# Two blocks of a transformer on one core: first conditioning pieces into the slab, ranks between the shared expert's halves, its down product in pair 14

## The chip, the core and the metric

The program runs on one core of a Trainium2 chip. The metric is the time of one execution on the device in microseconds. The kernel before took 2307.77 us in the median of three runs (2303.73 to 2310.81).

## The reference

256 tokens of width 1024, float32, pass through two blocks of two layers each. In the first block each layer is

```python
mod = silu(c) @ ada_w[layer] + ada_b[layer]
sh1, sc1, g1, sh2, sc2, g2 = split(mod, 6)
h = x * (1 + sc1) + sh1
y = mixer(h)                       # layer 0: block attention and gated linear attention; layer 1: gated delta rule
x = layer_norm(ALPHA * x + g1 * y)
h = x * (1 + sc2) + sh2
s = sigmoid(h @ router_w)          # 64 experts, top 6 of each token, limited to 4 of 8 groups
y = sum over a token's experts e of share_e * down_e(silu(gate_e h) * up_e h)
y = y + sh_down(silu(sh_gate h) * sh_up h)      # the shared expert, for all tokens
x = layer_norm(ALPHA * x + g2 * y)
```

The second block (attention with context and a pool mixer, then a Hyena and a Fourier mixer) follows on the same tokens. The change does not touch it.

## The kernel before

All weights come from HBM as pieces of 128 x 2048 float32, 1024 KB each. SP issues nearly all loads, in the order of the program and from one queue, into numbered buffers: four of `wbuf` (`NS = 4`) in the mixers, nine in the experts' stage (four of `wbuf`, two more of it, two of the slab, and `wP`). `load` takes the next buffer in turn and first waits until the work that held it is done; all later loads wait behind it. POOL issues the conditioning pieces of later sections on a queue of its own, into the two remaining pieces of `wbuf`.

**Conditioning.** `ada_w` is 12 sections for the first block, each of four pieces. VectorE multiplies a piece by its column of the activated condition and adds it up, two instructions a piece, eight a section (`ada_steps`). TensorE then sums over the partitions (`ada_pe`) and VectorE adds the bias (`ada_dve`). Sections 0 and 1 (shift and scale of the first layer) are summed at the start; SP loads their eight pieces with `load`, so the fifth waits for the first buffer. Sections 2 to 7 (`E_ADA`) are summed in the even mixer, a few steps at a time between the copies of the projections, with `some(steps, n)`. `ada_pool` issues each of their pieces when the one two before it has been summed.

**Start and even mixer.** VectorE makes h from x in eight pieces (`start_dve`), and one signal tells that all are made. `even_pe` first multiplies the table of relative position biases (33 x 4 by 512, `e_tab`), waits for that signal, then runs 13 projections of 256 columns (the last of 16), each 16 matrix products, and in the fourth, seventh, ninth and twelfth place after them an `ada_pe`. VectorE copies the bias table out first of all (L775), and POOL sends it through memory (`even_pool`) to lay it out as `hank`, which the scores need, and only then starts with section 2. After the projections come scores, softmax (with one conditioning step after each of its eight rounds), gated linear attention and the output product.

**Experts' stage** (`moe_sp`, `moe_pe`, `moe_act`, `moe_dve`), once a layer, at 264 to 830 us and 1242 to 1808 us. TensorE's order: router, transposes of h, gate and up products of the shared expert in two halves m (`m_sh`), the sums of the experts' places (`m_rank`), the shared down product into the accumulators `Y`, three gathers (`gather_pe`), then 32 pairs of experts. VectorE's order: the router's choice, the shared expert's two products silu(gate) times up (L1242), ranks (L974 on), two sets of places (`places_dve`, L311 and L1018), copies of the gathers. A gather needs its set of places. Pair q: gate and up of both experts, four pieces (L300), the scatter of pair q-1 into `Y`, transposes (L304), in the first nine pairs one more gather, and the down product from two pieces. ScalarE copies the rows of pair q+1 (`window_act`) while pair q runs.

In the trace one matrix product of `mm` is two records. L300 is the line of `mm`, L304 that of `tr`, L311 and L312 those of `ts`, L431 the conditioning sum.

## Time and profile before

| | |
|---|---|
| median of three runs | 2307.77 us |
| the profiled execution | 2311.57 us, its span 2309.7 us |
| TensorE products | 2039.2 us busy, 88% |
| VectorE | 814.7 us, 35% |
| ScalarE | 448.1 us, 19% |
| DMA | 577 MB, mean 250 GB/s |
| chain that ended last | PE 76%, DVE 10%, DMA 6%, issue 4% |

The page gives the whole; the change sits in three short stretches of it. So the views are read for those stretches: busy time of each engine by stage, the timeline around each edit, and for a transfer its issue, the time to its landing and the first instruction that reads it. A stage in which TensorE is busy without a gap can only lengthen if work is put into it; in one in which it waits, what it waits for decides.

### The profile page before, as it was taken

What the parts mean: (1) busy time and instruction counts of PE and PEld (TensorE: products, weight loads), DVE (VectorE), ACT (ScalarE), POOL (GpSimd) and SP (SyncE); (2) the same over time, 40 slices, a digit from 0 to 9 for tenths busy, and PEclk for the clock granted to TensorE, in tenths of its full rate; (3) what the DMA queues carried; (4) which work ended last, traced back from release to release, by engine and by line L of the source; (5) the groups of instructions that cost most, each with busy time, mean ns of one, the idle gap of its engine ahead of it and who ended that gap; (6) DMA issues with size and microseconds to landing.
All of it is one profiled execution on the core that took longest, in us unless ns stands there. A gap on an engine that the chain in (4) does not pass through costs nothing.

```text
span 2309.7 us, 24377 instructions
## 1 busy us (share of the span) xinstructions
PE 2039.2 (88%) x9590; PEld 1392.7 (60%) x9590; DVE 814.7 (35%) x1728; ACT 448.1 (19%) x982; POOL 84.8 (4%) x101
## 2 busy tenths in 40 slices
PE   5967899999999979958988999999999797779987
PEld 4856755554444458838977555444444585547856
DVE  4562353210111027668623622110111353551262
ACT  0013212112221221140022111212221403221021
POOL 0100000000000000010000000000000000020050
PEclk9976899999999989958988999999999898889999
DMA  9860278899999936863002788999999472112401
GB/s 368 327 252 7 90 309 332 355 386 405 407 411 410 407 144 252 302 250 110 1 23 86 302 355 356 383 409 407 406 413 407 190 291 73 32 55 74 146 21 37
DMA packets 80098, 576.99 MB, mean 250 GB/s; under 512 B 8925, under 2 KB 9181, under 8 KB 10529
## 3 DMA queue, kind: packets, MB, share of 16 engines
q1 hardware_dynamic: 68976, 494.84, 53.6%
q0 software_dynamic: 10992, 80.43, 9.5%
q8 instruction: 81, 1.33, 0.2%
q14 instruction: 49, 0.39, 0.0%
HBM read 574.17 MB, written 1.06 MB: 249 GB/s over the span
## 4 chain that ended last, share of the span: by engine, by line
PE 76%; DVE 10%; DMA 6%; issue 4%; ACT 2%; POOL 1%; POOLq 0%; SPq 0%; DVEq 0%; ACTq 0%
PE ps L300 75%; DMA wbuf<-in_ada 6%; DVE hma L431 4%; PE ps L304 2%; ACT slab L307 1%; DVE slab L311 1%; ACT L307 1%; POOL rs_t L2108 0%; POOL hma L2107 0%; DVE hma L312 0%; DVE slab L1018 0%; DVE slab L2263 0%; DVE slab L312 0%; POOL hma L2110 0%; DVE stat L1962 0%
## 5 line engine op out<-in xcount | busy, mean ns | idle before, releaser
L300 PE MATMUL ps<-slab 128*128 128x256 f32 (+5 forms) x2544 | 588.4, 405 | 29.0 <-issue 13.8
L300 PEld LDWEIGHTS ps<-slab 128*128 128x128 f32 (+2 forms) x2544 | 407.5, 186 | 186.7 <-issue 140.7
L307 ACT ACTIVATE slab<-ps 128x512 f32<-128x512 f32 (+3 forms) x282 | 148.2, 526 | 1290.5 <-PE ps L300 1278.5
L300 PE MATMUL ps<-wbuf,slab 128*64 128x512 f32 (+1 forms) x1392 | 349.9, 590 | 26.5 <-issue 26.5
L300 PE MATMUL ps<-hma,wbuf 128*128 128x256 f32 (+1 forms) x1648 | 368.0, 386 | 1.2 <-DVE hma L312 1.2
L300 PEld LDWEIGHTS ps<-hma,wbuf 128*128 128x128 f32 (+1 forms) x1648 | 317.2, 193 | 49.5 <-DVE hma L312 3.2
L300 PE MATMUL ps<-slab,cst 128*64 128x512 f32 (+3 forms) x554 | 187.0, 553 | 63.7 <-ACT slab L307 30.8
L300 PEld LDWEIGHTS ps<-wbuf,slab 128*64 128x64 f32 (+1 forms) x1392 | 122.5, 138 | 192.6 <-issue 191.8
L1264 DVE TENSOR_TENSOR slab<-ps,slab 128x256 f32<-128x256 f32 x64 | 27.2, 425 | 591.3 <-ACT slab L307 571.0
L431 DVE SCALAR_TENSOR_TENSOR hma<-wbuf,cs,hma 128x1024 f32<-128x1024 f32 x140 | 179.6, 1283 | 72.2 <-DMA wbuf<-in_ada 68.6
L300 PE MATMUL ps<-wbuf,cst 128*64 128x512 f32 x704 | 191.0, 592 | 0.0
L300 PEld LDWEIGHTS ps<-slab,cst 128*128 128x128 f32 (+1 forms) x554 | 93.2, 190 | 125.3 <-issue 79.2
L300 PE MATMUL ps<-wP,slab 128*64 128x512 f32 (+2 forms) x440 | 159.6, 484 | 8.9 <-DVE wP L1955 8.9
L300 PE MATMUL ps<-slab,wbuf 128*128 128x256 f32 x616 | 138.9, 388 | 11.9 <-DVE slab L879 8.8
L300 PEld LDWEIGHTS ps<-slab,wbuf 128*128 128x128 f32 x616 | 119.7, 195 | 32.3 <-issue 15.6
L300 PEld LDWEIGHTS ps<-wbuf,cst 128*64 128x64 f32 x704 | 65.9, 137 | 93.2 <-issue 92.9
L1269 DVE COPY slab<-ps 128x512 f32<-128x512 f32 x64 | 44.2, 691 | 202.5 <-PE ps L304 202.5
L304 PE MATMUL ps<-cst,slab 128*128 128x128 f32 x380 | 61.8, 297 | 36.0 <-DVE slab L311 12.4
L307 ACT ACTIVATE slab<-slab 128x512 f32<-128x512 f32 (+2 forms) x146 | 70.6, 509 | 104.5 <-DVE slab L580 85.3
L300 PEld LDWEIGHTS ps<-wP,slab 128*64 128x64 f32 (+1 forms) x440 | 62.9, 161 | 40.8 <-issue 30.5
L304 PEld LDWEIGHTS ps<-cst,slab 128*128 128x128 f32 x380 | 50.4, 154 | 48.4 <-issue 25.8
L300 PE MATMUL ps<-wbuf,hma 128*128 128x256 f32 (+2 forms) x256 | 56.5, 390 | 23.8 <-issue 15.9
(250 smaller groups left out, 1392.2 us busy)
## 6 DMA issues: line engine op xcount, KB each, us to landing
wbuf<-in_moe_gu SPq DMA_DIRECT2D x170, 1024.0 KB, 8.5
wbuf<-in_moe_d SPq DMA_DIRECT2D x88, 1024.0 KB, 10.3
wbuf<-in_ada POOLq DMA_DIRECT2D x72, 1024.0 KB, 5.7
slab<-in_moe_gu SPq DMA_DIRECT2D x64, 1024.0 KB, 8.6
wbuf<-in_od_in SPq DMA_DIRECT2D x30, 1024.0 KB, 4.9
wbuf<-in_ev_in SPq DMA_DIRECT2D x22, 1024.0 KB, 8.2
wP<-in_moe_gu SPq DMA_DIRECT2D x22, 1024.0 KB, 9.3
slab<-in_moe_d SPq DMA_DIRECT2D x20, 1024.0 KB, 10.3
```

The costliest lines, as they stand in the source:

```text
L300: return e.matmul(o, lhsT, rhs, start=start, stop=stop, skip_group_check=skip)
L304: return e.transpose(o, i, ident[0:n, 0:n])
L307: return e.activation(o, i, fn, bias=bias, scale=scale, accum_out=acc)
L311: return e.tensor_scalar(o, a, s1, None, op0)
L431: t = e.scalar_tensor_tensor(total, w, cs[:, c, k:k + 1], total, ALU.mult, ALU.add)
L1264: e.tensor_tensor(m_hh[:, q % 2, :], bank("m_gu", l, q)[:, 256:512], m_sg[:, q % 2, :], ALU.mult).then_inc(*V.up("m_hh", l, q))
L1269: e.tensor_copy(m_tp[:, q % 2, :], bank("m_tt", l, q)[:, :]).then_inc(*V.up("m_ttc", l, q))
```

## The change

The first eight conditioning pieces go to the slab, which is empty then, each with a semaphore of its own, without waiting for a buffer and ahead of x; the constants are loaded behind the second projection's weights. POOL issues the pieces of sections 2 and 3 as soon as the condition vector is made, ahead of the bias table's way through memory. Each of the eight pieces of h has a signal, and projection 0 waits for them one by one. The bias table's product and its copy move behind projection 3. In the experts' stage the sums of places stand between the two halves of the shared expert's gate and up; VectorE makes the second shared product between the first and the second set of places, and writes both to a free part of `hma`. The down product moves into pair 14, after the scatter, and its load to the place ahead of pair 14's loads. The first scatter opens the accumulators in its stead.

```diff
@@ -17,6 +17,7 @@
 ALPHA = float(4 ** 0.25)
 CAP = 64
 NC = 6
+SHARED_AT = 14

...
-        def proj_f(e, key, n, rhs, freed_by):
+        def proj_f(e, key, n, rhs, freed_by, ready=None):
             u = unit(key, 8, n)
             p = fill_bank(e, key, freed_by)
             e.wait_ge(*on("landed", key))
             for m in range((n + 127) // 128):
                 w = min(128, n - m * 128)
                 for k in range(8):
+                    if ready is not None and m == 0:
+                        e.wait_ge(*on(*ready(k)))
                     i = mm(e, p[0:w, m * 256:(m + 1) * 256], u[:, k, m * 128:m * 128 + w], rhs[:, k, :], k == 0, k == 7)
             i.then_inc(*P.up(*key))
             P.also("used", key)
...
         def ada_at(n, q):
-            return flat(unit(("ada", n, q), 1, 2048)) if n < 2 else wbuf[:, 4 + q % 2, :]
+            return S(4 * n + q, 2048) if n < 2 else wbuf[:, 4 + q % 2, :]

...
-                    V.also("used", ("ada", n, q))
+                    V.also("ada_used", n, q)
...
-        def ada_pool(e, tasks, *ready):
-            for x in ready:
-                e.wait_ge(*on(*x))
+        def ada_pool(e, tasks, first=True):
             for n in tasks:
                 for q in range(4):
-                    if n > tasks[0] or q > 1:
-                        e.wait_ge(*on("used", ("ada", n - (q < 2), (q + 2) % 4)))
+                    if n > tasks[0] or q > 1 or not first:
+                        e.wait_ge(*on("ada_used", n - (q < 2), (q + 2) % 4))
                     e.dma_start(wbuf[:, 4 + q % 2, :], A["ada"][TASKS[n][0], q]).then_inc(
                         *G.arrive(f"ada_w{q % 2}", ("ada", n, q)))
...
         def start_sp(e):
             e.dma_start(tab[:, :], A["table"]).then_inc(*Q.arrive("in_tab", "tab_in"))
-            e.dma_start(flat(xT[:, :, :]), A["xT"]).then_inc(*Q.arrive("in_x", "x"))
             for n in range(2):
                 for q in range(4):
-                    load(e, ("ada", n, q), A["ada"][n, q])
-            e.dma_start(cst[:, 0:lo], A["consts"][:, 0:lo]).then_inc(*Q.arrive("in", "in"))
+                    e.dma_start(ada_at(n, q), A["ada"][n, q]).then_inc(*Q.arrive(f"in_a{4 * n + q}", ("ada", n, q)))
+            e.dma_start(flat(xT[:, :, :]), A["xT"]).then_inc(*Q.arrive("in_x", "x"))
...
             for j in range(8):
-                i = ts(e, hT[:, j, :], xT[:, j, :], mc(0, 1, j), mc(0, 0, j), ALU.mult, ALU.add)
-            i.then_inc(*V.up("e_h"))
+                ts(e, hT[:, j, :], xT[:, j, :], mc(0, 1, j), mc(0, 0, j), ALU.mult, ALU.add).then_inc(*V.up("e_h", j))
             e.wait_ge(*V.now)
             ts(e, xT[:, :, :], xT[:, :, :], ALPHA, None, ALU.mult).then_inc(*V.up("x_scaled"))
...
         def even_sp(e):
             for i in range(12):
+                if i == 2:
+                    e.dma_start(cst[:, 0:lo], A["consts"][:, 0:lo]).then_inc(*Q.arrive("in", "in"))
                 load(e, ("e_proj", i), A["ev_in"][i])
             load(e, ("e_proj", 12), A["ev_glr"])
             load_out(e, "e_out", A["ev_out"])
...
         def even_pe(e):
-            p = fill_bank(e, ("e_tab",), ("e_tabc",))
-            e.wait_ge(*on("landed", "in"))
-            mm(e, p[0:4, :], rpe33, K("hot")[0:33, :], True, True).then_inc(*P.up("e_tab"))
-            e.wait_ge(*on("e_h"))
+            proj_f(e, ("e_proj", 0), 256, hT, ("e_ev", 0), lambda k: ("e_h", k))
             for i, (c0, n, f) in enumerate(E_UNITS):
-                (proj_f if f else proj_t)(e, ("e_proj", i), n, hT, ("e_ev", i))
+                if i:
+                    (proj_f if f else proj_t)(e, ("e_proj", i), n, hT, ("e_ev", i))
+                if i == 3:
+                    p = fill_bank(e, ("e_tab",), ("e_tabc",))
+                    e.wait_ge(*on("landed", "in"))
+                    mm(e, p[0:4, :], rpe33, K("hot")[0:33, :], True, True).then_inc(*P.up("e_tab"))
                 if i in (4, 7, 9, 12):
                     ada_pe(e, {4: 2, 7: 3, 9: 4, 12: 5}[i])
             for q in range(8):
...
         def even_dve(e):
-            e.wait_ge(*on("e_tab"))
-            e.tensor_copy(rs_t[0:4, 0, :], bank("e_tab")[0:4, :]).then_inc(*V.up("e_tabc"))
-
             def proj(i, dst, rows=128, cols=512, tokens=False):
                 e.wait_ge(*on("e_proj", i))
                 p = bank("e_proj", i)[0:rows, 0:cols]
@@ -786,6 +786,8 @@
                 *V.up("e_ev", 1))
             some(steps, 5)
             proj(3, flat(e_qk[:, 6:8, :]))
+            e.wait_ge(*on("e_tab"))
+            e.tensor_copy(rs_t[0:4, 0, :], bank("e_tab")[0:4, :]).then_inc(*V.up("e_tabc"))
             some(steps, 3)
             proj(4, e_v[:, :, 0:256], tokens=True)
             some(steps, 3)
...
-        m_sh = S(6, 2048)[:, 768:1792].rearrange("p (a n) -> p a n", a=4)
+        m_sh = S(6, 2048)[:, 768:1280].rearrange("p (a n) -> p a n", a=2)
+        m_shh = hma[:, 1:3, 1600:1856]
         m_htok = S(0, 2, 1024)
...
             if q == 1:
-                e.wait_ge(*on("m_shy", l))
+                e.wait_ge(*on("m_shv", l, 1))
...
             for j in range(8):
-                t = mm(e, Y(j), m_ys[:, q % 2, j * 128:j * 128 + 128], m_tp[:, q % 2, 256:512], False, q == NP - 1 and j % 2 == 1, True)
+                t = mm(e, Y(j), m_ys[:, q % 2, j * 128:j * 128 + 128], m_tp[:, q % 2, 256:512],
+                       q == 0 and j % 2 == 0, q == NP - 1 and j % 2 == 1, True)
             t.then_inc(*P.up("m_y", l, q))
...
         def moe_sp(e, l, before):
             load(e, ("m_rt", l), A["router"][l])
             load(e, ("m_shg", l), A["sh_gu"][l, 0])
             load(e, ("m_shu", l), A["sh_gu"][l, 1])
-            load(e, ("m_shd", l), A["sh_d"][l])
             slots.ids, slots.i = [slots.ids[(slots.i + i) % NS] for i in range(NS)] + list(range(NS, 9)), 0
             for s in range(NS, 9):
                 slots.held.pop(s, None)
             for q in range(NP):
+                if q == SHARED_AT:
+                    load(e, ("m_shd", l), A["sh_d"][l])
                 for part in (0, 4, "d"):
                     for x in (2 * q, 2 * q + 1):
                         key = ("m_w", l, x, part)
@@ -1106,6 +1111,26 @@
...
             slots.ids, slots.i = list(range(NS)), 0
             over(e, l, over_sp, Q)
 
+        def ranks_pe(e, l):
+
+            p = fill_bank(e, ("m_rank", l), ("m_rankr", l))
+            e.wait_ge(*on("m_msk", l))
+            mm(e, p[:, 0:64], K("before"), r_msk[:, 0, :], True, True)
+            mm(e, p[:, 64:128], ones, r_msk[:, 0, :], True, False)
+            mm(e, p[:, 64:128], K("before"), r_msk[:, 1, :], False, True)
+            mm(e, p[:, 128:192], ones, r_msk[:, 0, :], True, False)
+            mm(e, p[:, 128:192], ones, r_msk[:, 1, :], False, True).then_inc(*P.up("m_rank", l))
+
+        def shared_pe(e, l):
+            u = unit(("m_shd", l), 2, 1024)
+            e.wait_ge(*on("m_shv", l, 1))
+            e.wait_ge(*on("landed", ("m_shd", l)))
+            for kk in range(2):
+                for j in range(8):
+                    t = mm(e, Y(j), u[:, kk, j * 128:j * 128 + 128], m_shh[:, kk, :], False, False, True)
+            t.then_inc(*P.up("m_shy", l))
+            P.also("used", ("m_shd", l))
+
         def moe_pe(e, l, h):
 
             p = fill_bank(e, ("m_log", l), ("m_exp", l))
@@ -1125,6 +1150,8 @@
                         t = tr(e, p[:, k * 128:k * 128 + 128], hT[:, 4 * k2 + k, m * 128:m * 128 + 128])
                     t.then_inc(*P.up("m_ht", l, m, k2))
             for m in range(2):
+                if m:
+                    ranks_pe(e, l)
                 p = fill_bank(e, ("m_sh", l, m), ("m_shv", l, m))
                 for half, key in ((0, ("m_shg", l)), (1, ("m_shu", l))):
                     u = unit(key, 8, 256)
@@ -1135,23 +1162,7 @@
                     t.then_inc(*P.up("m_sh", l, m, half))
                     if m == 1:
                         P.also("used", key)
-
-            p = fill_bank(e, ("m_rank", l), ("m_rankr", l))
-            e.wait_ge(*on("m_msk", l))
-            mm(e, p[:, 0:64], K("before"), r_msk[:, 0, :], True, True)
-            mm(e, p[:, 64:128], ones, r_msk[:, 0, :], True, False)
-            mm(e, p[:, 64:128], K("before"), r_msk[:, 1, :], False, True)
-            mm(e, p[:, 128:192], ones, r_msk[:, 0, :], True, False)
-            mm(e, p[:, 128:192], ones, r_msk[:, 1, :], False, True).then_inc(*P.up("m_rank", l))
             take_y(e, ("y_res", f"m{l}"))
-            e.wait_ge(*on("m_shv", l, 1))
-            u = unit(("m_shd", l), 2, 1024)
-            e.wait_ge(*on("landed", ("m_shd", l)))
-            for kk in range(2):
-                for j in range(8):
-                    t = mm(e, Y(j), u[:, kk, j * 128:j * 128 + 128], m_sh[:, 2 + kk, :], kk == 0 and j % 2 == 0, False, True)
-            t.then_inc(*P.up("m_shy", l))
-            P.also("used", ("m_shd", l))
 
             e.wait_ge(*on("m_htc", l, 1, 1))
             for n in range(3):
@@ -1178,6 +1189,8 @@
                 P.also("m_gu", l, q, 1)
                 if q:
                     scatter_pe(e, l, q - 1)
+                if q == SHARED_AT:
+                    shared_pe(e, l)
                 p = fill_bank(e, ("m_tt", l, q), ("m_ttc", l, q))
                 e.wait_ge(*on("m_hh", l, q))
                 for i in range(2):
@@ -1237,12 +1250,15 @@
 
         def moe_dve(e, l):
             router_dve(e, l)
-            for m in range(2):
+            def shared(m):
                 e.wait_ge(*on("m_shs", l, m))
-                e.tensor_tensor(m_sh[:, 2 + m, :], bank("m_sh", l, m)[:, 256:512], m_sh[:, m, :], ALU.mult).then_inc(
+                e.tensor_tensor(m_shh[:, m, :], bank("m_sh", l, m)[:, 256:512], m_sh[:, m, :], ALU.mult).then_inc(
                     *V.up("m_shv", l, m))
+
+            shared(0)
             ranks_dve(e, l)
             places_dve(e, l, 0)
+            shared(1)
             places_dve(e, l, 1)
             for n in range(2):
                 gather_dve(e, l, n)
@@ -1790,7 +1806,8 @@
         def attn_pool(e):
             e.wait_ge(*on("m_gu", 1, NP - 1, 1))
             e.dma_start(cst[:, lo:], A["consts"][:, lo:]).then_inc(*G.arrive("c2", "late"))
-            ada_pool(e, A_ADA, ("n_c", "m1", 0))
+            e.wait_ge(*on("n_c", "m1", 0))
+            ada_pool(e, A_ADA)
 
         def attn_pe(e):
             rstd_pe(e, "ax", S(7, 8, 256))
@@ -2355,8 +2372,9 @@
         def pool_program(e):
             start_pool(e)
             e.wait_ge(*on("ca"))
+            ada_pool(e, E_ADA[0:2])
             even_pool(e)
-            ada_pool(e, E_ADA)
+            ada_pool(e, E_ADA[2:], False)
             delta_pool(e)
             attn_pool(e)
             hyena_pool(e)
```

## Rows read from the trace of the kernel before

**Rows 1.** The page of the kernel before: its first line.

```profile
span 2309.7 us, 24377 instructions
```

**Rows 2.** Busy time by stage: PE, PEld, DVE, ACT, POOL (instructions), granted clock, DMA share, GB/s.

```profile
0.00:36.90 36.90, 8.97 (x35) 7.09 (x35) 22.35 (x27) 1.51 (x2) 0.47 (x6) 1.00 0.97 398
36.90:138.00 101.10, 101.10 (x487) 87.49 (x488) 47.62 (x47) 3.67 (x5) 12.38 (x22) 1.00 0.89 334
...
484.40:829.80 345.40, 325.64 (x1518) 166.31 (x1516) 43.61 (x130) 70.54 (x194) 0.00 (x0) 1.00 0.96 391
```

**Rows 3.** Timeline of the start: start us, us, engine, line, instruction [idle before it].

```profile
9.67 0.75 DVE L311 TENSOR_SCALAR hma<-wbuf,cs 128x1024 f32<-128x1024 f32 x1 [9.67 <-DMA wbuf<-in_ada]
...
30.26 3.58 PE L300 MATMUL ps<-tab,hma 128*128 128x1 f32 x16 [6.54 <-DVE hma L431]
...
33.77 1.86 PE L300 MATMUL ps<-cst,tab 33*4 33x512 f32 x2
...
34.15 2.67 DVE L312 TENSOR_SCALAR hma<-xT,mods 128x256 f32<-128x256 f32 x8
...
36.87 3.35 PE L300 MATMUL ps<-hma,wbuf 128*128 128x256 f32 x7 [1.24 <-DVE hma L312]
```

**Rows 4.** DMA view of 2 to 37 us: packets, bytes and mean rate.

```profile
DMA packets 1994, 14.64 MB, mean 418 GB/s; under 512 B 215, under 2 KB 215, under 8 KB 328
```

**Rows 5.** DMA view of 50 to 56 us: packets, MB, share of 16 engines, by queue.

```profile
q0 software_dynamic: 180, 1.35, 58.1%
q1 hardware_dynamic: 141, 1.03, 40.7%
```

**Rows 6.** Timeline of VectorE alone in the projections' last third.

```profile
107.88 2.61 DVE L431 SCALAR_TENSOR_TENSOR hma<-wbuf,cs,hma 128x1024 f32<-128x1024 f32 x2 [1.58 <-DMA wbuf<-in_ada]
...
112.28 0.69 DVE L780 COPY slab<-ps 128x512 f32<-128x512 f32 x1 [0.37 <-PE ps L300]
...
146.06 2.60 DVE L431 SCALAR_TENSOR_TENSOR hma<-wbuf,cs,hma 128x1024 f32<-128x1024 f32 x2 [1.62 <-DMA wbuf<-in_ada]
```

**Rows 7.** Two of POOL's conditioning pieces, issued at 144.7 and 149.0 us.

```profile
DMA to landing us min/median/max: 5.1/5.1/5.1
```

**Rows 8.** Timeline between the first router and the first pair.

```profile
281.53 0.42 DVE L1242 TENSOR_TENSOR slab<-ps,slab 128x256 f32<-128x256 f32 x1 [2.72 <-ACT slab L307]
...
287.75 1.22 PE L300 MATMUL ps<-slab,cst 128*128 128x64 f32 x10
...
289.01 0.29 DVE L974 TENSOR_TENSOR slab<-ps,slab 128x128 f32<-128x128 f32 x1 [0.22 <-PE ps L300]
...
289.15 7.14 PE L300 MATMUL ps<-slab,wbuf 128*128 128x256 f32 x32 [0.18 <-issue]
...
297.33 0.62 DVE L311 TENSOR_SCALAR slab<-cst,rpl 128x256 f32<-128x256 f32 x2
...
297.40 10.60 PE L300 MATMUL ps<-slab 128*128 128x256 f32 x48 [1.10 <-issue]
...
309.26 7.09 PE L300 MATMUL ps<-wbuf,cst 128*64 128x512 f32 x32
```

**Rows 9.** Timeline: the transposes of two neighbouring pairs.

```profile
592.44 0.60 PE L304 MATMUL ps<-cst,slab 128*128 128x128 f32 x4
...
607.88 0.60 PE L304 MATMUL ps<-cst,slab 128*128 128x128 f32 x4
```

**Rows 10.** A gate and up piece issued at 585.5 us, and its first read.

```profile
DMA to landing us min/median/max: 9.2/9.2/9.2
...
600.79 0.59 PE L300 MATMUL ps<-slab 128*64 128x512 f32 x1
```

**Rows 11.** A gate and up piece issued at 330.1 us into an empty queue.

```profile
DMA to landing us min/median/max: 4.8/4.8/4.8
```

**Rows 12.** Busy time by stretch: PE, PEld, DVE, ACT, POOL, granted clock, DMA share.

```profile
137.40:140.90 3.50, 1.17 (x6) 0.69 (x4) 2.80 (x3) 0.00 (x0) 0.00 (x0) 1.00 0.84 356
140.90:144.30 3.40, 3.25 (x8) 2.52 (x8) 2.59 (x4) 0.00 (x0) 0.53 (x1) 0.50 0.55 176
```

## The prediction

> **What bounds the kernel now.** I read the page first [rows 1], then the busy time of each engine by stage [rows 2], because the change touches three stages with different limits. Up to 36.9 us TensorE is nearly idle (8.97 us busy) and waits for the conditioning sums on VectorE. From 36.9 to 138 us it is busy for all of its 101.10 us: the mixer's projections, one after the other. In the expert pairs without gathers (484 to 830 us) it is busy 325.64 of 345.40 us while the DMA engines show a share of 0.96: TensorE sets the pace and the weight transfers are right behind it. Then I read each place that the change edits in the order of time: the start [rows 3 to 5], the end of the projections [rows 6, 7], the stretch between router and first pair [rows 8], and a steady pair with its transfers [rows 9 to 11].
>
> **Part 1: the start.** The eight pieces of the first two conditioning sections go out at once, into the slab, and ahead of x. The first one takes x's place in the queue. One piece is 1024 KB = 1.049 MB, which at 418 GB/s [rows 4] is 2.5 us, so the first sum starts at 9.67 - 2.5 = 7.2 us instead of 9.67 [rows 3]. Against that stand POOL's two pieces of the next section, which the change now issues as soon as the condition vector is there, at about 5 us. A piece issued by POOL lands 5.1 us after its issue when nothing else is in flight [rows 7], 2.5 of these are the transfer, so they start to flow at about 7.5 us. With both queues full, POOL's had 58.1% of the engines' time and SP's 40.7% [rows 5]: I take an even split. Before the last of the eight can land, nine pieces (seven of SP's, two of POOL's) must pass after 7.2 us: 9 x 2.5 = 22.6, so 29.8 us. Its two sums take 2.6 us [rows 6], end 32.4. Today TensorE takes the last sums over at 30.26 [rows 3]; so they end 2.1 us later. x now comes after them, and lands at 32.3, before the sums are through TensorE (3.58 us more): it hides there, and so do SP's first two projection units, at 34.8 and 37.3 (the first is needed at 36.6, the second seven microseconds later).
>
> The first projection no longer waits for all eight pieces of h. Today h starts at 34.15 and TensorE at 36.87, so 2.7 us; after, TensorE needs only the first of eight pieces of 2.67 us, 0.3 us. It starts at 34.15 + 2.1 + 0.3 = 36.6 us: 0.3 us earlier. The small product of the bias table (two records, 1.86 us at 33.77, beside VectorE's work today) moves behind projection 3, into the busy stretch. These early records are slow ones: seven of the first projection take 3.35 us, 0.48 each [rows 3], against 7.14 / 32 = 0.22 us later [rows 8]. So it costs about half of 1.86, +0.9. TensorE then runs 0.6 us later up to 138 us. If its clock rises one step later than today, add up to 1.7 us.
>
> POOL's order changes too: the eight pieces of sections 2 and 3 are issued ahead of the bias table's round trip to memory, whose two transfers the scores need only after all projections; they leave some 50 us before that, hidden by the projections, and if that cover were gone the scores would wait for them. What is behind them is the first piece of section 4, some 2 us late against the new order but 4 us ahead of today's. VectorE's head start (the first pieces of section 2 are there when it is ready, where today it asks for them after the bias table) dies in the stretch behind: its sums are written between the copies of projections, and these follow TensorE. At 107.88 two sums wait 1.58 us for their piece [rows 6]; with the piece early they follow the copy before them, and gain 1.3 us. But at 112.28 VectorE waits for TensorE's projection 9, and the next sum stands behind it. From there POOL's two buffers set the pace (a piece is only asked for when the one two before it is summed) and the last two sums before the softmax end at 146.06 + 2.60 = 148.66 [rows 6]. I carry the 1.3 us less and the 0.6 us more to there: **-0.6 us** for the even stage. Its bounds: -5.2 (rival A) and +1.1 (late clock).
>
> **Part 2: between router and first pair, twice.** Today the order on TensorE is both halves of the shared gate and up, ranks (ten records, 1.22 us), shared down (32 records, 7.14 us), gathers. The gathers at 297.40 wait for VectorE's first places, which end at 297.33 [rows 8]. So the down product lay beside VectorE's work, and 1.10 us of idle time stood behind it. After, the ranks stand one half (6.9 us) earlier. VectorE's ranks start at 289.01 - 6.9 = 282.1; its chain of 8.3 us to the end of places 0 is unchanged, so 290.4. The first gather takes the bank of the second half, and VectorE frees that only with the second shared product (0.42 us), now placed after places 0: 290.9. Everything behind keeps its distances, since VectorE and TensorE shift together. The first pair starts 6.45 us before 309.26. The weights keep up, as SP no longer waits for the down product before it issues pair 0 and pair 1. **-6.45 us.** The windows' new wait, for the second shared product, is long over.
>
> **Part 3: the down product in pair 14, twice.** There nothing hides it: its 32 records are 6.9 us on the busiest engine: **+6.9 us**. Its piece is one more transfer in SP's queue, and it holds one of the nine buffers until pair 14. The third weight piece of pair 15 waits for that buffer, and all loads behind it wait with it on SP. A pair takes 607.88 - 592.44 = 15.44 us [rows 9]; the transposes start 10.95 us after its gate and up. So the down product runs from 10.95 to 17.85, SP issues at 18.2, and a load into an empty queue lands 4.8 us later [rows 11], at 23.0, the fourth at 25.5. TensorE wants that one half of a gate and up (3.43) into pair 15, at 15.44 + 6.9 + 3.43 = 25.8. Margin 0.3 us. Today's: issued 585.5, landed 9.2 us later at 594.7, first read 600.79, so 6.1 [rows 10]. The queue then hardly catches up: at 407 to 418 GB/s six pieces take 15.1 to 15.5 us of the 15.44. Zero to 4 us of stalls per layer; I take **+1.0**, near the low end, because rows 7 and 11 show that the single load is regular. By the Trainium skill ("DMA: Bandwidth & Descriptors", the anatomy of one DMA) a DMA costs about 2.0 us plus its bytes over 436 GB/s; an estimate from that is 4.4 us, which leaves a margin of 0.7 us, and the +1.0 would be nearly 0. The row says 4.8, and the sum goes by the row.
>
> **The sum.** -0.6 + 2 x (-6.45 + 6.9 + 1.0) = +2.3 us. The profiled execution took 2311.57 us (span 2309.7): 2313.9. The median of the three runs is 2307.77, 0.16% below it: **2310.1 us**.
>
> **Rivals.**
> A, POOL's pieces do not slow SP's. Rows 5 speak against it; for it, at 7 us SP's queue holds nine loads and POOL's two. Then the sums end at 7.2 + (30.26 - 9.67) = 27.8, TensorE starts 4.9 us earlier than today and 4.0 with the bias product counted: -5.2 with the 1.3, total 2305.5.
> B, the end on the slow side: the buffer held for pair 14. If the fourth piece of pair 15 comes over 0.3 us late, the margin is gone and each late landing up to pair 31 is paid, up to 4 us per layer: +8.3 in all, 2316.1.
> C, the clock. TensorE's idle time before the gathers grows from 1.1 to 2.1 us. Between 137.4 and 140.9 us it was busy 1.17 of 3.5 us and the next stretch was granted 0.50 [rows 12], which is the 1.2 GHz level. If that follows here, some 3.4 us run at half speed, 1.7 lost per layer: 2313.5.
> D, the head start lives: POOL's pieces land early enough that the softmax starts as TensorE allows, some 5 us earlier: 2305. Against it is the copy of projection 9 at 112.28.
> That the experts' part does nothing is nearly the forecast itself: the product changes its place between equals.
>
> **How the numbers follow.** Forecast 0.45, A 0.13, B 0.20, C 0.14, D 0.08. A measurement of this kernel can tell about 0.3%, 6.9 us, so 2300.8 and 2314.7 are the bounds of "same". Forecast, C and most of A and D lie between; A and D together without stalls reach 2300. B lies mostly above, and C with some stalls. Faster 0.12, same 0.67, slower 0.21. Range 2302 to 2317: A without stalls at the low end, B at the high one.
>
> **What would show it.** Right: first sum at about 7.2 us and its neighbours waiting for landings; TensorE's first projection at 36 to 37 us; softmax near 148; the first pair 6 to 7 us closer to its router; pair 14 at 22.3 us instead of 15.44; in pair 15 the first waits for a weight piece. Wrong: first projection at 32 us (A), TensorE waiting on in_moe_gu through pairs 15 to 31 (B), a granted 0.50 at the gathers (C), the softmax before 145 (D). A pair 14 under 20 us would mean that the loop had idle time that I did not see.

## The result and the profile after

The changed kernel takes **2313.96 us** (median of 20 runs, 2303.42 to 2325.75), the kernel before 2307.65 us in as many runs beside it: ratio 1.0028, 95% interval 1.0015 to 1.0040, that is 3.5 to 9.2 us slower, 6.5 in the middle. Forecast were +2.3 us, 2310.1, in a range of 2302 to 2317. The profiled execution took 2316.23 us with a span of 2314.4, 4.7 us longer than the span of before.

First the start, in the order of time (columns: start, duration, engine, line, operation, tiles, in brackets the idle time before it and what ended it):

```profile
7.11 0.75 DVE L312 TENSOR_SCALAR hma<-slab,cs 128x1024 f32<-128x1024 f32 x1 [7.11 <-DMA slab<-in_ada]
...
32.33 3.57 PE L301 MATMUL ps<-tab,hma 128*128 128x1 f32 x16 [7.04 <-DVE hma L434]
...
36.77 3.43 PE L301 MATMUL ps<-hma,wbuf 128*128 128x256 f32 x8 [0.87 <-DVE hma L313]
...
148.52 0.42 DVE L812 TENSOR_REDUCE stat<-ps 128x1 f32<-128x256 f32 x1
```

The first sum starts at 7.11 us instead of 9.67, the last sums are handed to TensorE at 32.33 instead of 30.26 [rows 3], and the first projection starts at 36.77. Behind that stand POOL's two early pieces, which share the engines with SP's eight (experiment 6 takes them away). The view of their line, issued at 5.1 and 5.8 us:

```profile
DMA to landing us min/median/max: 9.6/11.7/13.8
```

They took 9.6 and 13.8 us where one alone takes 5.1 [rows 7], and landed at 14.7 and 19.6 us, ahead of SP's last. The softmax begins 0.07 us before that of the kernel before (148.59).

Then the stretch from the first router to pair 0:

```profile
282.04 1.22 PE L301 MATMUL ps<-slab,cst 128*128 128x64 f32 x10
283.10 7.13 PE L301 MATMUL ps<-hma,wbuf 128*128 128x256 f32 x32
292.20 12.29 PE L301 MATMUL ps<-slab 128*128 128x256 f32 x48 [1.97 <-DVE hma L1255]
305.56 0.27 PE L305 MATMUL ps<-cst,rt 128*1 128x128 f32 x1 [1.07 <-DVE rt L999]
305.75 7.09 PE L301 MATMUL ps<-wbuf,cst 128*64 128x512 f32 x32
...
316.18 1.06 PE L305 MATMUL ps<-cst,slab 128*128 128x128 f32 x4 [3.34 <-DVE slab L1280]
317.04 4.90 PE L301 MATMUL ps<-slab 128*128 128x256 f32 x16
```

The ten records of 1.22 us, the sums of the experts' places (the ranks), lie between the two halves, the gathers start at 292.20 instead of 297.40, 27.5 us after the router's first record instead of 33.8. But the same 48 records take **12.29 us where before they took 10.60** [rows 8]. The windows of this stretch (busy time of PE, PEld, DVE, ACT, POOL, then the granted clock, DMA share, GB/s) show at what clock they ran:

```profile
290.00:292.00 2.00, 0.23 (x2) 0.00 (x0) 1.93 (x6) 0.38 (x1) 0.00 (x0) 1.00 0.89 246
292.00:293.00 1.00, 0.80 (x2) 0.74 (x3) 0.96 (x4) 0.00 (x0) 0.00 (x0) 0.66 0.75 311
293.00:295.00 2.00, 2.00 (x6) 1.56 (x5) 1.93 (x6) 0.00 (x0) 0.00 (x0) 0.50 1.05 438
295.00:297.00 2.00, 2.00 (x9) 1.67 (x9) 1.93 (x5) 0.00 (x0) 0.00 (x0) 0.82 0.98 414
```

TensorE stands still for 1.97 us, and from 293 to 295 us the granted clock is 0.50, the 1.2 GHz level. Once more in the same extract: behind the 3.34 us of idle time in pair 0 the transposes take 1.06 us and the 16 records of the next gather 4.90, where in pair 1 they take 0.60 and 3.62.

Last, pairs 14 and 15 of the first expert layer:

```profile
557.02 7.07 PE L301 MATMUL ps<-hma,wbuf 128*128 128x256 f32 x32
563.93 0.60 PE L305 MATMUL ps<-cst,slab 128*128 128x128 f32 x4
...
568.42 8.12 PE L301 MATMUL ps<-wbuf,slab 128*64 128x512 f32 x33
576.48 3.72 PE L301 MATMUL ps<-slab 128*128 128x256 f32 x16
580.03 0.60 PE L305 MATMUL ps<-cst,slab 128*128 128x128 f32 x4
```

From the transposes of the pair before to its own it is 22.34 us for pair 14 and 580.03 - 563.93 = 16.10 us for pair 15; all others from pair 10 on take 15.44 us, as in before [rows 9]. The view of `in_moe_gu`, the gate and up weights in HBM, has for the two pieces issued at 564.1 and 564.5 us, behind the buffer that the down product had held:

```profile
  PEld ps L301: 0.5, 1
...
DMA to landing us min/median/max: 4.8/6.6/8.4
```

The third came after 4.8 us, as reckoned, the fourth after 8.4, and TensorE's weight load waited 0.5 us. In the second layer the same two pieces took 4.9 and 7.0 us, and nobody waited.

Against before, the distance of the two executions at fixed points is: first router +1.15 us, gathers -5.20, pair 1 -4.54, pair 16 +3.03, second router +1.36, gathers -5.08, end of the second loop +3.89, end +4.66. So the first expert layer costs 1.9 us net and the second 2.5, and the rest is the start and what TensorE's clock does elsewhere. That last part moves by itself: behind the first expert layer 16 records of the same kind started 0.43 us apart in before and 0.22 apart in after, and 1.8 us came back with no part of the change at work.

### The profile page after: what moved, and what is told of

Same layout as the page of the kernel before. It is cut to its first block, busy times and chain, and to the rows that moved or that the text cites. A ratio compares the mean times of both kernels' runs of the same rounds, so it can differ in the third digit from the quotient of the medians.

```text
span 2314.4 us, 24378 instructions
## 1 busy us (share of the span) xinstructions
PE 2035.0 (88%) x9590; PEld 1388.8 (60%) x9590; DVE 815.5 (35%) x1728; ACT 448.2 (19%) x982; POOL 84.5 (4%) x101
## 3 DMA queue, kind: packets, MB, share of 16 engines
HBM read 574.17 MB, written 1.06 MB: 249 GB/s over the span
## 4 chain that ended last, share of the span: by engine, by line
PE 79%; DVE 9%; DMA 4%; issue 4%; ACT 2%; POOL 1%; SPq 0%; POOLq 0%; DVEq 0%; ACTq 0%
PE ps L301 77%; DMA wbuf<-in_ada 4%; DVE hma L434 2%; PE ps L305 2%; ACT slab L308 1%; DVE slab L312 1%; DMA slab<-in_ada 1%; DVE slab L1021 1%; ACT L308 1%; POOL rs_t L2125 0%; POOL hma L2124 0%; DVE slab L2280 0%; DVE slab L313 0%; POOL hma L2127 0%; DVE hma L313 0%
## 5 line engine op out<-in xcount | busy, mean ns | idle before, releaser
L301 PE MATMUL ps<-wbuf,slab 128*64 128x512 f32 (+1 forms) x1392 | 372.5, 590 | 26.5 <-issue 26.5
L301 PE MATMUL ps<-hma,wbuf 128*128 128x256 f32 (+1 forms) x1712 | 381.4, 385 | 0.9 <-DVE hma L313 0.9
L301 PEld LDWEIGHTS ps<-hma,wbuf 128*128 128x128 f32 (+1 forms) x1712 | 328.6, 193 | 48.4 <-issue 1.3
L301 PEld LDWEIGHTS ps<-wbuf,slab 128*64 128x64 f32 (+1 forms) x1392 | 127.4, 138 | 192.7 <-issue 190.6
L434 DVE SCALAR_TENSOR_TENSOR hma<-wbuf,cs,hma 128x1024 f32<-128x1024 f32 x126 | 161.7, 1283 | 57.8 <-DMA wbuf<-in_ada 54.6
L301 PE MATMUL ps<-wbuf,cst 128*64 128x512 f32 x704 | 170.9, 592 | 0.0
L301 PE MATMUL ps<-slab,wbuf 128*128 128x256 f32 x552 | 124.8, 389 | 11.6 <-DVE slab L881 8.8
L301 PEld LDWEIGHTS ps<-slab,wbuf 128*128 128x128 f32 x552 | 107.8, 196 | 30.2 <-issue 15.0
L301 PEld LDWEIGHTS ps<-wbuf,cst 128*64 128x64 f32 x704 | 61.2, 137 | 93.0 <-issue 92.6
```

Source lines behind the costliest of these rows:

```text
L301: return e.matmul(o, lhsT, rhs, start=start, stop=stop, skip_group_check=skip)
L434: t = e.scalar_tensor_tensor(total, w, cs[:, c, k:k + 1], total, ALU.mult, ALU.add)
```

## The experiments

They were run in three sets, each beside runs of the kernel before: experiments 1 to 4 without fill4 (before 2309.34 us), fill4 and 5 to 7 (2306.59), 8 to 10 (2307.06). So ratios, which are against these, can be compared between sets, and microseconds only within one. "Router to gathers" and the like are counted from the first record of the layer's router, so that what happens earlier does not enter.

**1 and 2. Each part alone (moe_only, start_only).** moe_only takes back the edits in proj_f, ada_at, ada_pool, start_sp, even_sp, even_pe, even_dve and pool_program, and keeps the experts' part. start_only does the opposite. The main lines of the two edits, against the kernel after, moe_only first:

```diff
-            ada_pool(e, E_ADA[0:2])
             even_pool(e)
-            ada_pool(e, E_ADA[2:], False)
+            ada_pool(e, E_ADA)
```

```diff
+            load(e, ("m_shd", l), A["sh_d"][l])
...
-                if q == SHARED_AT:
-                    shared_pe(e, l)
```

> The kernel before with the experts' part of the change alone (ranks between the two halves of the shared gate and up, down product in pair 14); the start is as before. Theory 1 (TensorE's clock): the first gathers come about 6.4 us nearer to their router, but behind some 2 us of idle TensorE they run at the lower clock, so that the 48 gather products take 12.3 us instead of 10.6; with 6.9 us for pair 14 and 0 to 0.7 us of stall that is +2.2 to +2.9 us per layer, 2312 to 2314 us. Theory 2 (the start carries the excess over my sum): the experts' part gives about 0 to +2 us in all, 2308 to 2310 us.

> The kernel before with the start's part of the change alone (slab pieces, POOL's two early pieces, h piece by piece, bias product behind projection 3); the experts' part is as before. Theory 1: within 1.2 us of before, the softmax starts within 0.7 us of 148.6 us, and nothing in the experts' part moves against its router. Theory 2: 3 us or more slower than before.

moe_only: 2315.74 us, ratio 1.0024 (1.0008 to 1.0039), 1.7 us above its range of 2312 to 2314, beside a before of 2309.34. start_only: 2309.12 us, ratio 1.0003 (0.9987 to 1.0018), as its first theory said. The loss is that of the experts' part; the start is worth nothing that these runs can tell from zero. Within moe_only the gathers come 27.5 and 27.9 us after the router and take 2.73 us for the first six where full clock gives 1.3; from gathers to first pair it is 13.55 us in both layers, in before 11.86. Pair 14 takes 22.35 and 22.34 us, pair 15 16.17 and 15.44, and pair 16 of the second layer 15.52.

start_only's profile was taken in its slowest execution, misses the expected softmax (within 0.7 us of 148.6) by 6 us and shows a weak spot. Its POOL pieces issued at 85.7 and 86.6 us (who waited for them, us and times, then issue to landing):

```profile
  DVE hma L311: 9.4, 1
  DVE hma L433: 1.9, 1
...
DMA to landing us min/median/max: 10.1/11.6/13.1
```

and TensorE some 15 us later:

```profile
113.48 2.06 PE L300 MATMUL ps<-tab,hma 128*128 128x1 f32 x16 [1.08 <-DVE hma L433]
115.40 19.16 PE L300 MATMUL ps<-hma,wbuf 128*128 128x256 f32 x80
```

VectorE waited 9.4 us for a piece, TensorE then 1.08 us for VectorE, and its next 80 records took 19.16 us where after needs 17.62. The softmax of this one execution started at 155.24 us; in the seven others with the changed start and POOL's early pieces it started between 148.5 and 150.7, median of all eight 149.3, against 147.6 to 148.8 in the three executions with the old start. So the middle is some 0.7 us later and one in eight was late by 6; with three executions on the other side neither is firm.

**3. The idle time filled (fill, fill4).** Products that nothing reads, directly ahead of the first gather:

```diff
             e.wait_ge(*on("m_htc", l, 1, 1))
+            for j in range(9):
+                mm(e, Y(0), K("before"), m_htok[:, 0, 0:256], True, True, True)
             for n in range(3):
```

> The kernel after, with nine products of 256 columns (nothing reads them) on TensorE directly ahead of the first gather, in both expert layers: 9 x 0.216 = 1.94 us of work in the 1.97 us in which it stood idle. Theory 1 (the idle time brings the clock down): the 48 gather products take 10.6 us again, not 12.3, their start does not move by more than 0.2 us, and the whole is some 3.3 us faster than after, 2310 to 2311 us. Rival (the clock falls there for another reason, such as the work before it): the gathers still take 12.3 us and the time is after's, 2314 us.

2317.52 us, ratio 1.0031 (1.0018 to 1.0044): no gain, where 3.3 us were expected. The profile shows an error of mine and an answer all the same:

```profile
288.98 4.05 PE L301 MATMUL ps<-slab,cst 128*128 128x256 f32 x18
292.87 10.52 PE L301 MATMUL ps<-slab 128*128 128x256 f32 x48
```

A product is two records, so nine were 4.05 us of work in a gap of 1.97. The gathers are back at 10.52 us and start 2 us late: what the clock gave, the filling took. So it was repeated with four, which leaves the rest of the kernel as it was:

> The kernel after with four products of 256 columns (eight records, 1.7 us; nothing reads them) on TensorE ahead of the first gather of both expert layers, where the run with nine of them had shown 18 records, 4.05 us, twice what fits. Theory 1 (the 2 us of idle time bring the clock down, and only that): gathers start 27.5 us after their router's first record as in after, take 10.5 us instead of 12.3, and the first pair starts 39.3 us after the router instead of 41.0; 3.4 us faster than after in all, 2310 to 2311 us if after is 2314. Rival (the clock falls in a stretch that the eight records do not cover, or something else starts late): first pair at 41 us behind the router, time as after.

```profile
289.67 1.89 PE L301 MATMUL ps<-slab,cst 128*128 128x256 f32 x8
291.80 10.60 PE L301 MATMUL ps<-slab 128*128 128x256 f32 x48 [0.24 <-DVE hma L1257]
303.47 0.27 PE L305 MATMUL ps<-cst,rt 128*1 128x128 f32 x1 [1.07 <-DVE rt L999]
303.67 7.09 PE L301 MATMUL ps<-wbuf,cst 128*64 128x512 f32 x32
314.10 0.63 PE L305 MATMUL ps<-cst,slab 128*128 128x128 f32 x4 [3.34 <-DVE slab L1282]
314.56 3.62 PE L301 MATMUL ps<-slab 128*128 128x256 f32 x16
```

The gathers start at the same distance from the router (27.4 us, second layer 27.9) and take 10.60 us, and the first pair starts 39.3 and 39.8 us after the router instead of 41.0 and 41.5. The eight records cover most of the idle time and change nothing else, so the idle time is what costs 1.7 us per layer here. The whole is less clear: 2310.65 us, ratio 1.0020 (1.0004 to 1.0036), an interval that overlaps after's; a gain in the total is not shown. Pair 0 differs between the two layers as well: in the first the clock stayed up behind its 3.34 us of idle time (the last two lines; 18.02 us from its transposes to those of pair 1), in the second the pair took 20.78 us, where after has 19.70 and 19.71.

**4. The down product in front of the gathers (down_front).** In moe_sp the piece is loaded behind the shared gate and up again, and in moe_pe the call moves:

```diff
             take_y(e, ("y_res", f"m{l}"))
+            shared_pe(e, l)
...
-                if q == SHARED_AT:
-                    shared_pe(e, l)
```

> The kernel after with the down product taken out of pair 14 and put back in front of the gathers (its transfer again behind the shared gate and up); the ranks stay between the two halves. Theory 1: TensorE is busy up to the first gather, so no fall of the clock; the gathers start some 1.6 us nearer to their router than in before; pair 14 takes 15.44 us and pair 15 has no stall: 2 x -1.6 us and after's start, 2304 to 2306 us. Rival (the loop had idle time for the product, or the clock falls anyway): no faster than before, 2308 us or more.

2315.2 us, ratio 1.0033 (1.0019 to 1.0048), a miss: I had left VectorE's second shared product behind places 0, and the down product waits for it.

```profile
293.52 8.83 PE L300 MATMUL ps<-hma,wbuf 128*128 128x256 f32 x32 [2.08 <-DVE hma L1252]
302.19 10.52 PE L300 MATMUL ps<-slab 128*128 128x256 f32 x48
...
1273.26 7.14 PE L300 MATMUL ps<-hma,wbuf 128*128 128x256 f32 x32 [2.08 <-DVE hma L1252]
```

The idle time is now ahead of the down product, and again the records behind it are slow (8.83 us for 7.14). In the second layer (the last line) the same 2.08 us of idle time went by without a fall, and so did the 3.34 us in its pair 0 (18.03 us), so gaps of these sizes do not bring it every time. What the down product costs in front of the gathers with no idle time ahead of it, this run does not show; experiment 8 does.

**5. Pair 6 instead of pair 14 (at6).**

```diff
-SHARED_AT = 14
+SHARED_AT = 6
```

> The kernel after with the down product and its piece in pair 6 instead of pair 14, where the pairs still hold gathers and take 18.0 us each, so that the weight queue has 2.5 us to spare in every pair. Theory 1 (the held buffer costs little): pair 6 takes 24.9 us, no stall behind it, against 0 to 0.7 us behind pair 14: 0 to 1 us faster than after. Rival (the held buffer and the full queue carry the excess of after): 3 to 5 us faster than after, and a narrower spread of its times.

2314.07 us, ratio 1.0024 (1.0011 to 1.0037). Pair 6 takes 24.90 us in both layers, and no pair behind it is a hair longer than in before. The stalls are gone and the ratio is that of after (1.0028) within the intervals: rival B is not what made it slow.

**6. POOL behind the eighth piece (pool_late).**

```diff
             e.wait_ge(*on("ca"))
+            e.wait_ge(*on("landed", ("ada", 1, 3)))
             ada_pool(e, E_ADA[0:2])
```

> The kernel after, with POOL waiting for the landing of the eighth conditioning piece before it issues its own two. Theory (the even split of the two queues): sums of the first two sections end at 27.8 us instead of 32.3, TensorE's first projection at 32 to 33 us instead of 36.8; but the softmax starts no earlier than 148 us, because the chain of POOL's two buffers and VectorE sets it: within 1.5 us of after in all. Rival: the 4 to 5 us live on to the softmax, 2309 to 2310 us where after has 2314.

```profile
27.57 3.57 PE L301 MATMUL ps<-tab,hma 128*128 128x1 f32 x16 [6.54 <-DVE hma L434]
...
32.02 2.47 PE L301 MATMUL ps<-hma,wbuf 128*128 128x256 f32 x5 [0.87 <-DVE hma L313]
...
145.30 0.42 DVE L812 TENSOR_REDUCE stat<-ps 128x1 f32<-128x256 f32 x1
```

TensorE takes over the last sums at 27.57, and the first projection starts at 32.02: the prediction's count of nine pieces with POOL's and seven without is right, to 0.3 us. POOL's two pieces had cost SP's eight 32.33 - 27.57 = 4.8 us, about two transfers' time. That both passed ahead of SP's last is shown; that the shares of the two queues were equal meanwhile is not. The Trainium skill ("DMA: Bandwidth & Descriptors", "SWDGE vs HWDGE vs iDMA") has each DMA engine take turns between the two kinds of queue; the traces agree as far as they go, 4.8 us for two pieces that were issued early. The second half of the expectation fell: the softmax starts at 145.30, not 148. In time 2310.72 us, ratio 1.0014 (1.0001 to 1.0028); against after's 1.0028 (1.0015 to 1.0040) the intervals overlap, and its rival with 2309 to 2310 us is nearer than the theory.

**7. The down product in two halves (split_down).** The first half needs only the first shared product and stands in front of the gathers; the second stands in pair 0, where TensorE waits for VectorE. The piece's buffer goes to the end of the ring of nine, since otherwise pair 0's own weights would wait for it.

```diff
+            load(e, ("m_shd", l), A["sh_d"][l])
+            first = [slots.ids[(slots.i + i) % NS] for i in range(NS)]
+            slots.ids, slots.i = first[:3] + list(range(NS, 9)) + first[3:], 0
...
             take_y(e, ("y_res", f"m{l}"))
+            shared_pe(e, l, 0)
...
-                if q == SHARED_AT:
-                    shared_pe(e, l)
+                if q == 0:
+                    shared_pe(e, l, 1)
```

> The kernel after with the down product out of pair 14: its first half (16 records, 3.45 us, needs only the first shared product) directly ahead of the gathers, its second half in pair 0, where TensorE waits 3.34 us for VectorE between gate and up and the transposes. Its piece is loaded behind the shared gate and up, into the buffer that comes round last. Theory 1: clock stays up; gathers start 28.8 us after the router's first record and take 10.5 us, the transposes of pair 0 come at 50.9 us (after 51.4, before 56.1 to 56.7), pair 14 takes 15.44 us: some 5.5 us per layer less than before, 2297 to 2300 us. Rival (the third weight piece of pair 1, now behind the held buffer, comes late, or pair 0 waits for weights): some us lost again in pair 1, 2303 us or more.

```profile
284.48 10.58 PE L300 MATMUL ps<-hma,wbuf 128*128 128x256 f32 x48
294.89 10.52 PE L300 MATMUL ps<-slab 128*128 128x256 f32 x48
...
306.68 7.09 PE L300 MATMUL ps<-wbuf,cst 128*64 128x512 f32 x32
313.70 3.72 PE L300 MATMUL ps<-hma,wbuf 128*128 128x256 f32 x16
317.26 0.60 PE L304 MATMUL ps<-cst,slab 128*128 128x128 f32 x4
317.70 3.62 PE L300 MATMUL ps<-slab 128*128 128x256 f32 x16
```

**2297.43 us**, ratio 0.9959 (0.9944 to 0.9974), inside the expected range. No bracket of idle time from the shared gate and up to the gathers, none ahead of the transposes of pair 0, and all at full clock. From its transposes to those of pair 1, pair 0 takes 17.99 us in both layers (after 19.70, before 20.73 and 19.33), which I had not reckoned with.

**8. Both halves in front (both_front)**, to see whether it is the places that count:

```diff
             shared_pe(e, l, 0)
+            shared_pe(e, l, 1)
...
-                if q == 0:
-                    shared_pe(e, l, 1)
```

> The kernel of split_down with the second half of the down product moved from pair 0 to directly behind its first half, ahead of the gathers. Theory (a record is free only where TensorE waits for another engine anyway): the first half fills the 2 us of idle time, the second delays the gathers by its 3.45 us, to 32.2 us behind the router, and pair 0 has its 3.34 us of idle time back, so the transposes of pair 0 come at 54.5 us (split_down 51.1, before 56.1); if the clock falls in that idle time, pair 0 takes 19.7 us instead of 18.0. 3.3 to 5.0 us per layer slower than split_down, 2304 to 2307 us. Rival (split_down gained from the earlier weights or the free buffer, not from the places of the halves): within 2 us of split_down.

```profile
284.62 14.03 PE L300 MATMUL ps<-hma,wbuf 128*128 128x256 f32 x64
298.49 10.52 PE L300 MATMUL ps<-slab 128*128 128x256 f32 x48
...
320.70 0.63 PE L304 MATMUL ps<-cst,slab 128*128 128x128 f32 x4 [3.34 <-DVE slab L1282]
321.17 5.31 PE L300 MATMUL ps<-slab 128*128 128x256 f32 x16
```

2307.22 us, ratio 0.9997 (0.9981 to 1.0012), as the kernel before and at the upper end of what was expected. Pair 0's idle time is back, and with it the slow records (5.31 us for 3.62).

**9 and 10. Two halves with another start (split_pool_late, split_old_start)**: split_down with the wait on POOL of experiment 6, and split_down with the old start, that is with the edits of moe_only in the first diff above.

> split_down and pool_late together: the down product in two halves, and POOL's first two pieces behind the eighth of SP's. Theory: the lead of the start (4.8 us at the first projection) is cut to some 3 us at the softmax by the chain of POOL's two buffers, and stays: 2293 to 2296 us. Rival (the lead is lost before the router, because the softmax stage waits for the next conditioning sums): 2297 to 2298 us, as split_down.

> split_down with the start of the kernel before. Theory (the start's part of the change is worth nothing at the softmax): within 1.5 us of split_down, 2296 to 2299 us, softmax at 148.6 us as in before. Rival (the start's part helps or hurts by its own): 2 us or more to either side.

split_pool_late: **2289.17 us**, ratio 0.9922 (0.9900 to 0.9945), the fastest, and 4 us below its expected range; softmax at 143.49 us. split_old_start: 2293.61 us, ratio 0.9945 (0.9925 to 0.9965), softmax at 147.60. This is a miss too: within 1.5 us of split_down was expected, and by the ratios it is some 3 us faster, with a softmax 2.4 us earlier than split_down's 149.96. That is the rival's "2 us or more", but the two intervals overlap (split_down 0.9944 to 0.9974), so that the change's start costs something without the wait on POOL is suggested and not shown; that it is any help without it, no run shows. With the wait, the new start is 4.4 us faster than the old one in the same set; five of its six executions lie below all eight of split_old_start, though the intervals of the ratios still overlap.

## Why the forecast held, and where it was off

**The time fell into the range, but the sum was a third of what was measured** (+2.3 against +6.5 us, interval 3.5 to 9.2). The places and prices of the moved work were right; a fall of the clock that costs 3.4 us had no term. That the range held owes something to luck: its upper end was set by rival B, which did not occur, and stalls reckoned 1.3 us too high made up for part of the clock. By its steps:

- *Gathers 6.45 us nearer to the router.* Measured 33.81 - 27.46 = 6.35 us in the first layer and 6.45 in the second. Right, the bank that VectorE frees only behind places 0 included: the row of the gathers names L1255, that product.
- *"Everything behind keeps its distances."* This is the step that failed. The 48 gathers became 1.69 us longer in each layer. Rival C had named it, with the place, the level and the price of 1.7 us, and got 0.14; its sign of being wrong, a granted 0.50 at the gathers, came. It occurred in all eight layers of the four profiled kernels that had the 1.97 us gap there (after, moe_only, pool_late, at6), 13.55 us from gathers to first pair each time, and in none of the four with the gap filled (fill and fill4, 11.78 to 11.87 us). C's own time was 2313.5; the median is 2313.96, so near because stalls too high and a start too low cancel in it. The rows that I had [rows 12] showed a fall behind 2.3 us of idle time, and none behind the 1.10 us of [rows 8]. The kernel before also had a fall that no row shows, in its pair 0 behind 3.34 us of idle time (the line below this list). The gap that the change opens lies nearest to the first of these three, and the chance should have been the larger one.
- *+6.9 us in pair 14.* 22.34 us in both layers instead of 15.44. Right.
- *+1.0 us of stalls.* 0.66 us in the first layer, none in the second; in moe_only 0.73 (pair 15) and 0.08 (pair 16), so 0.37 in the mean of four layers. The mechanism was as told (SP issues at the end of the down product, third piece after 4.8 us), the size a third of mine, and it came by the fourth piece. Rival B's "each late landing up to pair 31 is paid" did not occur, and the run with pair 6 shows that it was not the loss. The estimate of 4.4 us that the prediction set beside its row, from the Trainium skill ("DMA: Bandwidth & Descriptors", the anatomy of one DMA), rests on a fit that the section makes for transfers issued by POOL; these loads are SP's, and the third pieces took 4.8 and 4.9 us.
- *Pair 0* had no term. Behind its 3.34 us of idle time the clock falls as well, in 18 of the 20 profiled layers that have this gap, for longer or shorter: 20.73 and 19.33 us in before, 19.70 and 19.71 in after, 18.0 without a fall. Between these two executions it gives -1.0 and +0.4.
- *The start, -0.6 us.* 32.4 us for the last sums (measured 32.33) and 36.6 for TensorE (36.77) held. Carried to the softmax it gave -0.07 in the profile and +0.7 in the median of eight. The 1.3 us that VectorE was to gain at 107.88 were 0.8 (the sum behind the copy starts at 110.38 instead of 111.16), and the wait for projection 9 at 112.29 took them, where the prediction had carried them on to the softmax.
- *"From there POOL's two buffers set the pace."* Too strong, and not tested by the change itself. With TensorE 4.8 us earlier (pool_late) the softmax came 3.2 us earlier than after's, 4.0 than the median. That VectorE's sums, which stand between the copies of the projections, mostly follow TensorE would explain it; no run separates that from the rest. Rival A's 4.9 us for TensorE's first projection were right (4.85 against before), of its 5.2 us in all 3.3 had come at the softmax (148.59 - 145.30), and its condition, undisturbed transfers, does not hold while both queues are full.

Pair 0 of the kernel before, behind its idle time (columns as in the windows above, the granted clock third from the end):

```profile
318.40:325.20 6.80, 5.51 (x15) 4.62 (x16) 2.56 (x6) 0.00 (x0) 0.00 (x0) 0.50 0.90 380
```

With 1.69 for the clock, 0.37 for the stalls in place of 1.0 and 6.40 for the gathers the experts' part is 2 x (-6.40 + 1.69 + 6.9 + 0.37) = +5.1 us, less 0.6 for pair 0, and the start +0.7: +5.2, inside the interval. The single execution's +4.7 us of span is the same within what the clock moves elsewhere. What is not settled is why a gap of 2 us brings the clock down ahead of the gathers every time and ahead of the down product in experiment 4 once in two, and why pair 0's fall is long in one execution, short in another and missing in two.

## What to carry to other kernels

A product costs nothing only in a place where its engine waits for another one: look for the idle brackets in the timeline and give each a piece of work that fits and is ready by then, in halves if need be. Here the down product cost its full 6.9 us in pair 14, where TensorE waited for next to nothing; in two halves in gaps of 2.0 and 3.3 us it delayed the gathers by 1.4 us in the first layer and 0.7 in the second, pair 0 by nothing more, and both falls of the clock were gone. When a change brings a consumer forward, read how long its engine will then stand idle before it, and price the clock behind the gap as well as the gap. And an early transfer on a second queue takes its share of the engines: here two pieces that nobody needed yet delayed the last of the urgent ones by 4.8 us, their full length.

## What the runs showed of the hardware

- 1.97 us of idle TensorE, behind 9 us of unbroken work at full clock (281 to 290 us in after), were followed by the 1.2 GHz level in eight of eight cases: 1.69 us lost on 48 records. With 1.89 us of filling and 0.24 us of idle time there was no fall in two of two, and behind 1.06 to 1.10 us of idle time (before, start_only) none in four of four. Behind 2.08 us it was one of two, behind pair 0's 3.34 us 18 of 20.
- An f32 product of 256 columns is two records of 0.216 us at full clock (nine products were 18 records).
- A POOL piece of 1024 KB that takes 5.1 us alone took 9.6 and 13.8 us against SP's full queue, and up to 13.1 us between the projections' transfers (start_only).
- The time of one kernel moves by 10 to 20 us between executions (after 2303 to 2326), and the granted clock with it: after's two fastest executions, 2303.42 and 2304.85 us, had a mean clock of 0.942, its slowest, 2325.75 us, 0.931. split_down spread over 3.5 us in six runs, split_pool_late over 8.0; whether it moves less is not shown by so few.
